# Ranking by comparison, a re-cut last group, and two groups of four experts moved to third and fourth place in a decoder step

## The reference, cut to what matters

```python
gprob = softmax(xt @ router_g + router_g_b); gp, gidx = top_k(gprob, 1)        # 4 groups
elog  = take(xt @ router_e + router_e_b, gidx)                                  # 8 experts of that group
ev, eidx = top_k(elog, 2); wts = gp * softmax(ev); eid = gidx * 8 + eidx
gate = sum(one_hot(eid, 32) * wts[..., None], axis=1)
for wg, wu, wd, ge in experts:                                                  # 32 of them
    acc += ge[:, None] * ((silu(xt @ wg) * (xt @ wu)) @ wd)
y = rmsnorm(h + acc, norm_f_w)
```

## Time and profile before

| what | value |
|---|---|
| median of 3 runs | 846.13 us (845.77 to 849.34) |
| the profiled execution's own time | 846.87 us |
| its span | 845.0 us |
| mean granted TensorE clock | 0.985 of full speed |
| moved | 248.07 MB, mean 294 GB/s |

### The profile page before, as it was taken

One profiled execution on the slowest core, in us unless ns is written; L12 is line 12 of the kernel. 1 busy time (PEld: TensorE's weight loads), 2 busy tenths in 40 slices (PEclk: granted clock), 3 DMA queues, 4 the chain that ended last, 5 costly groups with the idle time before them and its releaser, 6 DMA issues.

```text
span 845.0 us, 13493 instructions
## 1 busy us (share of the span) xinstructions
PE 806.6 (95%) x5406; PEld 486.8 (58%) x5406; DVE 478.7 (57%) x1269; ACT 165.7 (20%) x323; POOL 30.4 (4%) x89
## 2 busy tenths in 40 slices
PE   9999999999999999999999899999999999999795
PEld 7657777787667667775454353554355355444252
DVE  6377899864559685236793443662463265247233
ACT  3342011346321330023111010111011011111013
POOL 0000302500010000000000000000000000000000
PEclk9999999999999999999999999999999999999798
DMA  7223253233433503999999999999999999999992
GB/s 293 100 93 103 78 173 128 85 127 130 151 121 119 167 14 111 398 431 400 415 425 384 426 427 426 428 425 428 426 426 427 428 427 426 426 427 426 425 396 76
DMA packets 30337, 248.07 MB, mean 294 GB/s; under 512 B 3488, under 2 KB 4768, under 8 KB 17088
## 3 DMA queue, kind: packets, MB, share of 16 engines
q1 hardware_dynamic: 30272, 247.17, 72.3%
HBM read 242.23 MB, written 4.92 MB: 292 GB/s over the span
## 4 chain that ended last, share of the span: by engine, by line
PE 63%; DMA 25%; DVE 8%; issue 2%; ACT 1%; SPq 0%; DVEq 0%
PE psum L1234 17%; DMA sb_arena<-w_gu 17%; PE psum L648 13%; DMA sb_spare<-w_gu 8%; PE psum L659 5%; PE psum L1118 4%; PE psum L1170 4%; PE psum L1283 3%; PE psum L1089 2%; DVE sb_arena L1861 1%; DVE sb_arena L1858 1%; PE psum L969 1%; PE psum L1164 1%; PE psum L630 1%; PE psum L804 1%
## 5 line engine op out<-in xcount | busy, mean ns | idle before, releaser
L1234 PE MATMUL psum<-sb_arena 128*64 128x512 f32 (+1 forms) x1216 | 247.2, 600 | 15.4 <-DMA sb_spare<-w_gu 7.9
L1234 PEld LDWEIGHTS psum<-sb_arena 128*64 128x64 f32 (+1 forms) x1216 | 80.7, 130 | 167.2 <-issue 143.6
L648 PE MATMUL psum<-sb_arena 128*128 128x313 f32 (+2 forms) x480 | 127.3, 424 | 0.1
L2345 DVE TENSOR_TENSOR sb_arena<-sb_arena,psum 128x512 f32<-128x512 f32 x14 | 9.6, 688 | 183.7 <-PE psum L1234 183.7
L648 PEld LDWEIGHTS psum<-sb_arena 128*128 128x128 f32 x480 | 90.0, 190 | 34.9 <-issue 2.3
L2328 DVE STREAM_TRANSPOSE sb_arena<-sb_arena 32x128 f32<-32x128 f32 x224 | 68.0, 303 | 3.6
L659 PE MATMUL psum<-sb_arena 128*128 128x288 f32 x256 | 67.8, 419 | 0.0
L1234 PE MATMUL psum<-sb_constant,sb_arena 128*64 128x512 f32 (+1 forms) x144 | 65.7, 610 | 2.1 <-DMA sb_spare<-w_gu 2.1
L1234 PE MATMUL psum<-sb_spare,sb_arena 128*64 128x512 f32 (+1 forms) x144 | 65.7, 610 | 0.0
L659 PEld LDWEIGHTS psum<-sb_arena 128*128 128x128 f32 x256 | 48.4, 194 | 16.5 <-issue 3.7
L2338 DVE STREAM_TRANSPOSE sb_arena<-sb_arena 32x64 f32<-32x64 f32 (+1 forms) x224 | 54.9, 245 | 2.9
(11 more groups left out here) (421 smaller groups left out, 857.7 us busy)
## 6 DMA issues: line engine op xcount, KB each, us to landing
sb_arena<-w_gu SPq DMA_DIRECT2D x48, 2048.0 KB, 35.8
sb_arena<-w_dn SPq DMA_DIRECT2D x20, 2048.0 KB, 35.1
sb_arena<-w_in SPq DMA_DIRECT2D x30, 512.0 KB, 3.4
sb_constant<-w_gu SPq DMA_DIRECT2D x6, 2048.0 KB, 32.1
sb_spare<-w_gu SPq DMA_DIRECT2D x6, 2048.0 KB, 36.6
sb_arena<-w_gab SPq DMA_DIRECT2D x16, 512.0 KB, 3.4
sb_arena<-w_gu SPq DMA_DIRECT2D x8, 1024.0 KB, 8.7
sb_constant<-w_dn SPq DMA_DIRECT2D x3, 2048.0 KB, 34.5
```

What stands on the lines that cost most here:

```text
L648: last = mm(bk(n % 2, N)[:, first_col(n):], w_ring[n % 2][:, k, :], (xw if n < 2 else xnT)[:, k, first_col(n):], start=(k == 0), stop=(k = ...
L1234: last = mm(bank[b][own_, :], rows[:, k, own_], weights(s, k), start=(k == 0), stop=(k == of - 1))
```

## The change

1. `first_of` goes. For each token, two 8x8 tables say which other logit is larger, or equal and earlier (new constant `earlier`); a sum over a row of them is the logit's rank. `taken` is rank below 1.5; `member` goes (the last tile's count uses 32 of its rows). The two maxima and the difference `m2 - m1` come later, the difference after `flag`.
2. `gate_units` are placed two at a time between `spread_rows`' matmuls; two of them also stand after the column transposes. Their number is the same.
3. The groups' order: pair, pair, four, four, then ten pairs. The last group is a pair.
4. The down loads of the first two experts of the third group wait for a down half each, instead of the whole down product, and come in halves.
5. The last group's program: `combine` and `turn_tokens` come before the gate product, the up product is in two halves (their loads too, with semaphores of their own), 16 dummies stand between the halves, the hidden rows are turned by TensorE transposes and taken out by ScalarE, and the dummies are counted 4, 16, 4 and 14.
6. The second row tile of `y` is stored from ScalarE's queue. One more dummy stands before the position matmuls.

```diff
-        SIZES = (2, 2, 4, *[2] * 10, 4)
+        SIZES = (2, 2, 4, 4, *[2] * 10)
-        FIRST_RANK = (0, 2, 24, *range(4, 24, 2), 28)
+        FIRST_RANK = (0, 2, 24, 28, *range(4, 24, 2))
...
+                        if (i, part) == (2, 2):
+                            for n in range(2):
+                                sp.wait_ge(S["sp_dn"], 3 + n)
+                                for s in range(2):
+                                    load_piece(2, 2, s, experts[s], n * HOME // 2, (n + 1) * HOME // 2)
...
+                            if (i, part) == (LAST, 1):
+                                load_piece(i, part, s, e, 0, HOME // 2, "ld_half_up")
...
+                for s, e in enumerate(experts):
+                    load_piece(LAST, 1, s, e, HOME // 2, HOME)
                 product, n = freed_by(3 * E - 1 - AHEAD)
                 sp.wait_ge(S[product], n)
-                for landing, q in (("ld_dn1", slice(0, 2)), ("ld_dn0", slice(2, 3)), ("ld_up0", slice(3, 4))):
+                for landing, q in (("ld_dn1", slice(0, 2)), ("ld_third", slice(2, 3)), ("ld_fourth", slice(3, 4))):
...
-                gate_product(LAST)
+                pe.wait_ge(S["xe"], 4 * LAST + 4)
                 for j in range(KD):
                     combine(LAST, EARLY_COMB, j)
                 spread_norm()
                 pe.wait_ge(S["sp_acc"], KD * LAST + 2)
                 for m, n in ((0, 0), (0, 1), (0, 2), (1, 0)):
                     turn_tokens(m, n)
+                pe.wait_ge(S["norm_row"], NC + 1)
+                turn_tokens(1, 1)
+                gate_product(LAST)
+                keep_warm(4, 4)
                 pe.wait_ge(S["sp_silu"], GROUPS)
                 for n in range(3):
                     turn_tokens(2, n)
-                pe.wait_ge(S["norm_row"], NC + 1)
-                turn_tokens(1, 1)
-                keep_warm(8, 4)
-                up_product(LAST)
+                up = lambda s, k: home(LAST, 1, s)[:, k, :]
+                pe.wait_ge(S["ld_half_up"], 16 * 6 + LAST_LANDED)
+                project(LAST, 1, xe, up, range(0, 4), KD)
+                keep_warm(16, 4)
+                pe.wait_ge(S["ld_up1"], landed_by(LAST, 1))
+                project(LAST, 1, xe, up, range(4, KD), KD).then_inc(S["sp_up"], 1)
+                keep_warm(4, 4)
                 pe.wait_ge(S["sp_hid"], GROUPS)
+                for k in range(4):
+                    last = pe.transpose(bank[4][:, k * P:k * P + P], hid_s[:, k * P:k * P + P], K("ident"))
+                last.then_inc(S["hid_tr"], 1)
                 turn_tokens(1, 2)
-                keep_warm(16, 4)
+                pe.wait_ge(S["hidT"], GROUPS)
+                keep_warm(14, 4)
                 pe.wait_ge(S["ld_dn1"], landed_by(LAST, 2))
-                pe.wait_ge(S["hidT"], GROUPS)
                 down_product(LAST, 0).then_inc(S["sp_dn"], 1)
...
+            TT(above, other, mine, ALU.is_gt)
+            step(TT(level, other, mine, ALU.is_equal))
+            step(TT(level, level, over(earlier, 3), ALU.mult))
+            step(TT(above, above, level, ALU.add))
+            step(V.tensor_reduce(oh1, above, AX.X, ALU.add))
+            step(TS(oh2, oh1, 1.5, None, ALU.is_lt))
+            TT(taken.rearrange("p m (g e) -> p m g e", g=G), spread(ohg, EG), oh2.unsqueeze(2).to_broadcast([P, 3, G, EG]), ALU.mult)\
+                .then_inc(S["rt_member"], 1)
...
-            spread_rows(0)
-            gate_units(38, 46)
-            spread_rows(1)
-            gate_units(46, 54)
+            gate_units(36, 38)
+            spread_rows(0, 38)
+            gate_units(42, 46)
+            spread_rows(1, 46)
+            gate_units(50, 54)
```

More of the change, by code:

```diff
@@ L67 @@
 CST = Cols()
-for _name, _n in (("ident", P), ("ones", P), ("eps", 1), ("first8", 8), ("before", P), ("before_in", P), ("iota", CAP), ("valid", 3), ("quarter", 4), ("fold", 36),
+for _name, _n in (("ident", P), ("ones", P), ("eps", 1), ("first8", 8), ("earlier", EG * EG), ("before", P), ("before_in", P), ("iota", CAP), ("quarter", 4), ("fold", 36),
                   ("blockones", P), ("center", P), ("sum_r", B32), ("spread_r", P), ("hot", 2 * B32), ("spread_g", 2 * P), ("row_g", HG * P),
@@ L130, in constants @@
     put("perm", perm)
-    put("valid", i[:, None] + P * np.arange(3)[None] < M)
+    eg = np.arange(EG)
+    put("earlier", np.tile((eg[None] < eg[:, None]).reshape(1, -1), (P, 1)))
     return c
@@ L300, in build @@
         rt8 = [r.take(3, EG) for _ in range(4)]
+        above, level = r.take(3, EG, EG), r.take(3, EG, EG)
         rt4 = r.take(3, G)
@@ L303, in build @@
         gate = r.take(3, E2)
-        member = r.take(3, E)
         taken = r.take(3, E)
@@ L352, in build @@
         AHEAD = len(ring)
+        LAST_LANDED = 16 * SIZES[LAST]
         def flat_home(i, part, s):
@@ L363, in landed_by @@
         def landed_by(i, part):
-            in_pieces = 64 if part == 2 and i % 2 or part == 0 and i % 2 == 0 and i else 0
+            in_pieces = 64 if part == 2 and i % 2 or part == 0 and i % 2 == 0 and i else 32 if part == 2 and i >= 2 else 0
             return 16 * sum(SIZES[i % 2:i + 1:2]) + in_pieces
@@ L425, in tokens @@
             return bank[PIECE_BANKS[m][n]][slice(0, P) if m < 2 else slice(B32 * n, B32 * n + B32), 0:hi - lo]
-        for name, same_as in (("norm_diag", "o_gated"), ("norm_row", "o_sb"), ("second_out", "z_done"), ("row_sum", "conv_step"), ("piece", "moe_done")):
+        for name, same_as in (("norm_diag", "o_gated"), ("norm_row", "o_sb"), ("second_out", "z_done"), ("row_sum", "conv_step"), ("hid_tr", "kv_tr"),
+                              ("ld_half_up", "ld_oa0"), ("ld_third", "ld_oa1"), ("ld_fourth", "ld_oa2"), ("piece", "moe_done")):
             S[name] = S[same_as]
@@ L562, in expert_at, with load_piece @@
                 return sp.value_load(ids[0:1, r:r + 1], min_val=0, max_val=E - 1)
-            def load_piece(i, part, s, e, lo, hi):
+            def load_piece(i, part, s, e, lo, hi, landing=None):
                 of = (dram["w_gu"][bass.ds(e, 1), :, part].rearrange("a p k c -> p (a k c)") if part < 2
                       else dram["w_dn"][bass.ds(e, 1)].rearrange("a p q k c -> p (a q k c)"))
-                sp.dma_start(flat_home(i, part, s)[:, lo:hi], of[:, lo:hi]).then_inc(S[f"{parts[part]}{i % 2}"], 16)
+                sp.dma_start(flat_home(i, part, s)[:, lo:hi], of[:, lo:hi])\
+                    .then_inc(S[landing or f"{parts[part]}{i % 2}"], 16)
             def load_by_rank():
@@ L616, in _ @@
                 load_by_experts()
-            for m, ready, n in ((0, "out_ready", 2), (1, "second_out", 2), (2, "out_ready", 3)):
-                sp.wait_ge(S[ready], n)
+            for m, n in ((0, 2), (2, 3)):
+                sp.wait_ge(S["out_ready"], n)
                 sp.dma_start(dram["y"][m * P:min(m * P + P, M)], out_tok[m]).then_inc(S["stores"], 16)
@@ L895, in _, with spread_rows @@
             last.then_inc(S["cols_tr"], 1)
-            def spread_rows(p):
+            def spread_rows(p, first):
                 if p:
@@ L905, in spread_rows @@
                 last.then_inc(S["g_bc"], 1)
+                gate_units(first, first + 2)
                 for h, rows_, _ in pair:
@@ L908, in spread_rows @@
                 last.then_inc(S["g_bc"], 1)
+                gate_units(first + 2, first + 4)
                 for h, _, _ in pair:
@@ L1146, in _ @@
                     last.then_inc(S["xt_tr"], 1)
-            for _ in range(8):
+            for _ in range(9):
                 mm(bk(4, P), K("ones"), K("ones"), start=True, stop=True)
             pe.wait_ge(S["rt_member"], 1)
[L1151 to L1155, removed]
+            mm(bank[6][:, 0:2 * E], K("before"), taken[:, 0:2, :], start=True, stop=False)
+            mm(bank[6][:, 2 * E:3 * E], K("before_in"), taken[:, 2, :], start=False, stop=False)
+            mm(bank[6][:, E:3 * E], K("ones"), over(taken[:, 0, :], 2), start=False, stop=False)
+            mm(bank[6][:, 2 * E:3 * E], K("ones"), taken[:, 1, :], start=False, stop=True).then_inc(S["rt_pos"], 1)
+            mm(bk(7, 2 * E), K("ones"), taken[:, 0:2, :], start=True, stop=False)
+            last = mm(bank[7][:, 2 * E:3 * E], K("ones")[0:B32], taken[0:B32, 2, :], start=False, stop=True)
             last.then_inc(S["rt_pos"], 1)
@@ L1257, in down_quarter @@
                         for s in range(SIZES[LAST]):
-                            own_ = slice(s * B32, s * B32 + B32)
+                            own_ = slice(s * P // SIZES[LAST], (s + 1) * P // SIZES[LAST])
                             last = mm(bank[4][own_, 0:256], hidT[:, k, own_], home(LAST, 2, s)[:, q, k, :], start=(k == 0), stop=(k == 3))
@@ L1597, in finish @@
                 A(out_tok[1], out_tok[1], ACT.Copy, scale=total[:, 1:2]).then_inc(S["second_out"], 1)
+                act.wait_ge(S["second_out"], 2)
+                act.dma_start(dram["y"][P:2 * P], out_tok[1]).then_inc(S["stores"], 16)
             def dense():
@@ L2173, in _ @@
```

(13 more changed lines are left out.)

16 lines of the change are left out of this document (9 added, 7 removed).

## The result

The changed kernel takes **867.7 us** (median of 4 runs, 866.93 to 868.69) against 845.95 (845.68 to 849.34): a ratio of 1.0252, 95% interval 1.0228 to 1.0277. Predicted were 864.0 us, range 860 to 870. The profiled execution took 868.69 us, 1.0 above the median; its span is 866.9 us, where the prediction's sum gave 862.75 for a span: 4.15 us too little.

A forecast was written before the change was run, and what follows sets the result against it. Transfers were taken to lead TensorE by little, with TensorE's lag behind them paid once, at the last group: 846.13 + 22.35 (lag, stores included) - 4.6 (gains in the weight stream) = 863.9 us, range 860 to 870.

The forecast's parts named there:

- The lag: At the last group, now a pair: TensorE's delay behind the transfers is paid there, +22.35 us with 0.9 saved on stores.
- The 22.47 us: Group 12: least time from the landing of its up weights to the end of the group, 22.47 us.
- the 35.1: Last group: 35.1 us from the end of group 12 to its first down half, with no wait for a transfer.
- the first rival: Whole-kernel end: TensorE keeps up and the transfers set the end, median 833 us; chance 6%.
- The rival of the dry ring: In the two fours: TensorE frees the ten homes late, transfers dip 2.15 us each time, 868 to 870 us; chance 8%.
- (a): Before the weight stream: gate units strewn between `spread_rows`' matmuls keep the faster pace, saving 1.7 us, bounds 0 and 1.7.
- (b): Router comparisons before the position matmuls: shorter, giving back 0.9 us of the transfer dip at 393 to 400 us.
- (c): Third group's first down loads: issued 3.5 us earlier in halves, closing the transfer dip at 446 to 450 us, saving 2.0.
- The stores: Kernel end: one store on ScalarE's queue removes an issue from SP's, saving 0.9 us, bounds 0 and 1.9.

## Why the prediction was right, and where it was not

**The lag (+22.35 us): right, by its own steps.** With the stores in it, as in the forecast, the term measured 24.2 us (81.57 from the 88th load to the end of the span, for 57.38 before); 1.6 of the difference are at the end (below). The 88th load releases group 12's up product instead of the last gate product. The 22.47 us measured 22.44 and the 35.1 measured 35.41. Within the latter the errors are small and cancel: the dummies cost 9.34 instead of 8.5 (4 of them 1.09, not 0.90), `turn_tokens`' 28 records 3.12 instead of 2.77; against that its 16 records took 1.03 instead of 1.58 and the transposes 0.45 instead of 0.79. The order alone gives 19.5 us, and undoing it gives back 27.5: both sides of the same mechanism, with the old last group and with the new one, which is 3.45 us slower behind a pair. In the profiles the order alone moves the first down half by 16.3 us (821.94 to 838.25), and undoing it by 27.6 (843.18 to 815.62).

**What bounds the end: right, against the rule.** The Trainium skill (Perfetto Trace Analysis, section Identifying the Most-Contended Engine) does not take matmul busy time as the measure of how close TensorE is to its limit, but the busy share of weight loads, together with the arithmetic done as a share of the peak (MFU), which the prediction left out and no run here shows. In the 22.44 us of group 12 weight loads are busy for 11.63 us and matmuls for all of it, and none of it could be caught up. Read by the weight loads alone TensorE would have been half free, and the trace does not agree with that; the first rival, 833 us, fell with it: the transfers do end at 824 to 825, and the kernel ends 42 us later. The rival of the dry ring fell too; the fours ran at 426 to 429 GB/s.

**(a) The parted rows (-1.7 us): the step that failed.** The prediction took the difference of 5.77 and 4.08 us as a property of what stands before the strip. It is not: it comes from a granted clock of 0.50 in part of the strip, which comes and goes between executions, whole or parted. Parting costs 2.3 us and gains nothing that a run shows. Its bounds, 0 and 1.7, did not even hold the sign, because the row matmuls and the gate units between them were costed at nothing above their old durations, though the two strips of row matmuls ran side by side before and every record got new neighbours. Without this term the sum would have been 865.6 us; with whole rows 865.08 was measured. That the two are so near is in part luck: the stream gained 1.4 us more than predicted, and the end lost 1.6.

**(b) The comparisons (-0.9 us): right in kind,** 1.15 measured by the timeline and some 1.5 in the transfers from 386 to 460 us; no run undoes them alone. **(c) The halves (-2.0 us): the mechanism right,** the dip is gone and comes back without them; 2.0 us in the transfers, but the size in the time stays open. Together with the dip at 393 us the stream gained 4.3 us for 2.9; the stream of the order alone, with neither part, was already 1.5 us shorter than that of before (451.2 for 452.6), so 1.4 us more is within what two executions differ by.

**The stores (-0.9 us): not there.** From VectorE's last scaling to the end of the span it was 5.66 us before and 6.41 after. Over the profiles the six with the store on ScalarE have 5.5 to 6.6 and the four with all on SP 5.7 to 6.5. In the two profiles what is saved on one issue is lost in the hold of another. From the first down half to that scaling it was 17.31 us (17.40 before), so all of the +1.6 at the end is here: 0.9 not saved and 0.75 more.

## What to carry to other kernels

Where transfers lead an engine by a little, look at which group comes last: the engine's lag behind the transfers is paid there once, in full, unless the last group's own transfers take longer than its work. A difference between two strips of one profiled execution is no property of the code until a second execution has it too. When matmuls of unlike shapes are strewn among each other, cost each of them at a duration beside its new neighbours, and look in the timeline whether two of them ran side by side.

## What the runs showed of the hardware that was not expected

- Two strips of matmuls with a stationary operand of 4 rows, one on rows 0 to 3 and one on rows 32 to 35, start 0.02 us apart when they follow each other and take 0.69 us together; when 288-column matmuls part them they take 1.37 us.
- In the stretch of small matmuls at 204 to 240 us the granted clock falls to 0.50 for some 3 us in some executions and stays at 1.00 in others, of either form (16 records 5.77 or 4.08 us). Strewing large matmuls among the small ones did not prevent it.
- In nine of ten profiles one of the last three stores is held at its issue: alone it takes 1.0 to 2.3 us instead of 0.4, or two of them 1.87 and 2.22, with either arrangement of queues. Its cause is open.
